# Two transformer blocks on one core: the elementwise work of GpSimd is given to VectorE

## The reference, cut to what matters

```
shift, scale, gate = split(c @ mod_w + mod_b, 3)
h = rms_norm(x, w0) * (1 + scale) + shift
x = x + gate * rms_norm(part(h), w1)          # part: mixer_ab, swiglu, mixer_cd, swiglu
```

## Time and profile before

| | |
|---|---|
| median of three runs | 1168.1 us |
| profiled execution, first to last instruction | 1171.9 us (no other time of it is given) |
| busy: TensorE, VectorE, ScalarE, GpSimd | 1064.7, 807.0, 509.4, 292.7 us |
| low parts on VectorE (line 1003) | 182, 296.7 us in all |
| low parts on GpSimd (line 621) | 91, 242.0 us in all |
| shared jobs on GpSimd (line 654) | 7, 24.0 us in all |
| pair sums on GpSimd (line 471) | 22, 17.8 us in all |

### The profile page before, as it was taken

How to read it: one execution, slowest core, us unless ns; L and a number is a source line. 1 busy time by engine, 2 the same in 40 slices (tenths; PEclk the granted TensorE clock), 3 DMA queues, 4 the chain that set the end, 5 groups by cost and what they waited for, 6 DMA issues and landing times.

```text
span 1171.9 us, 20802 instructions
## 1 busy us (share of the span) xinstructions
PE 1064.7 (91%) x8107; PEld 1010.4 (86%) x8107; DVE 807.0 (69%) x1043; ACT 509.4 (43%) x859; POOL 292.7 (25%) x128
## 2 busy tenths in 40 slices
PE   1788799989999998999979999998989789999996
PEld 1687677979999997988979999997977789999995
DVE  4771657676777756768776777756596687667765
ACT  1421255345444344546344344444641345555454
POOL 2220134122323332220123223331210122232222
PEclk9898799899999999999989999999995899999999
DMA  9889532336677762880527776763753245544540
GB/s 380 284 270 167 187 140 83 92 142 244 254 288 272 266 218 100 294 331 14 178 74 252 270 290 250 265 215 117 253 209 114 95 169 172 184 162 162 180 159 36
DMA packets 58410, 229.44 MB, mean 196 GB/s; under 512 B 6384, under 2 KB 8432, under 8 KB 57840
## 3 DMA queue, kind: packets, MB, share of 16 engines
q1 hardware_dynamic: 58352, 228.64, 56.2%
HBM read 227.04 MB, written 1.57 MB: 195 GB/s over the span
## 4 chain that ended last, share of the span: by engine, by line
PE 58%; DVE 18%; ACT 9%; DMA 7%; issue 6%; SPq 1%; POOL 0%; DVEq 0%; ACTq 0%; POOLq 0%
PE bank L1562 15%; PE bank L1564 14%; PE bank L1563 14%; DMA modbuf<-in_mod_w 5%; DVE wL L1003 4%; DVE acc L485 4%; ACT wH L703 3%; DMA raw<-in_weights 2%; PE bank L1578 2%; PE bank L1648 2%; ACT pr L802 2%; DVE pr L1191 1%; PE bank L1796 1%; PE bank L1678 1%; PE bank L1765 1%
## 5 line engine op out<-in xcount | busy, mean ns | idle before, releaser
L1562 PE MATMUL bank<-hH,wH 128*128 128x256 f32 x1632 | 472.4, 289 | 18.3 <-DVE hL L1051 14.0
L1563 PE MATMUL bank<-hL,wH 128*128 128x256 f32 x1632 | 464.7, 285 | 0.0
L1564 PE MATMUL bank<-hH,wL 128*128 128x256 f32 x1632 | 464.5, 285 | 0.0
L621 POOL TENSOR_TENSOR wL<-raw,wH 128x1024 fp32r<-128x1024 f32 x91 | 242.0, 2659 | 748.4 <-ACT wH L703 748.4
L1003 DVE TENSOR_TENSOR wL<-raw,wH 128x1024 fp32r<-128x1024 f32 x182 | 296.7, 1660 | 90.6 <-ACT wH L703 90.4
L1562 PEld LDWEIGHTS bank<-hH,wH 128*128 128x128 f32 x1632 | 316.1, 194 | 28.0 <-issue 16.5
L1563 PEld LDWEIGHTS bank<-hL,wH 128*128 128x128 f32 x1632 | 316.5, 194 | 0.2
L1564 PEld LDWEIGHTS bank<-hH,wL 128*128 128x128 f32 x1632 | 316.1, 194 | 0.0
L703 ACT ACTIVATE wH<-raw 128x1024 fp32r<-128x1024 f32 x273 | 273.5, 1048 | 79.6 <-PE bank L1564 46.3
L1562 PE MATMUL bank<-aH,wH 128*128 128x256 f32 x528 | 149.5, 283 | 2.1 <-DVE aL L1202 2.1
L1563 PE MATMUL bank<-aL,wH 128*128 128x256 f32 x528 | 149.4, 283 | 0.0
(11 more groups left out here) (237 smaller groups left out, 1186.0 us busy)
## 6 DMA issues: line engine op xcount, KB each, us to landing
raw<-in_weights SPq DMA_DIRECT2D x273, 512.0 KB, 4.6
modbuf<-in_mod_w SPq DMA_DIRECT2D x48, 768.0 KB, 5.1
modbuf<-in_w_ada SPq DMA_DIRECT2D x32, 768.0 KB, 5.3
modbuf<-in_mod_w SPq DMA_DIRECT2D x14, 512.0 KB, 9.6
strips<-in_cmp_w SPq DMA_DIRECT2D x4, 512.0 KB, 10.9
strips<-bias_table SPq DMA_DIRECT2D x8, 256.0 KB, 11.3
otok<-in_mod_w SPq DMA_DIRECT2D x3, 512.0 KB, 15.4
acc<-in_mod_w SPq DMA_DIRECT2D x2, 512.0 KB, 11.2
```

Source lines behind the costliest of these rows:

```text
L621: nc.gpsimd.tensor_tensor(wL[:, slot, :], raw[:, slot, :], wH[:, slot, :].bitcast(F32), ALU.subtract).then_inc(lo_ready[2], 1)
L1562: mm(out, lhs_h, rhs_h, start=start, stop=False, skip_group_check=True)
L1563: mm(out, lhs_h, rhs_l, start=False, stop=False, skip_group_check=True)
L1564: return mm(out, lhs_l, rhs_h, start=False, stop=stop, skip_group_check=True)
```

## The change

GpSimd keeps its clearing and loses the rest. `split_upto` on VectorE makes the low parts of all three classes, and the loop's step makes the third one behind `aL`, ahead of the job. `add_pairs` runs over all four chunks on VectorE; for A0 it stands before the last starting job. The seven shared jobs are ordinary jobs, one in every third step of the attention, behind `take_pt` and `add_o`; ScalarE's `scale_half` goes. GpSimd's `split_low`, `pairs` and its part of the jobs are taken out. No load, no matmul and no buffer is changed.

```diff
         def jobs_done(phase, e):
             if phase == "ab":
-                return JOBS_AT_START + min(KT, e + 1) + min(SHARED_JOBS[0], max(0, e - 9))
+                return JOBS_AT_START + min(KT, e + 1) + min(4, max(0, e - 9))
...
-        def add_pairs(eng, tensor_tensor, norm, chunks=range(4)):
+        def add_pairs(eng, tensor_tensor, norm):
             n = NORMS.index(norm)
-            for b in chunks:
+            for b in range(4):
                 buf = squares_buffer(n, b)
                 eng.wait_ge(sq_ready, 4 * n + b + 1)
-                if b == 3:
-                    eng.wait_ge(pair_ready, 4 * n + 3)
                 tensor_tensor(buf[:, 0:S], buf[:, 0:S], buf[:, S:2 * S], ALU.add).then_inc(pair_ready, 1)
...
         def _(pool):
-            def split_low(b, i=None):
...
-            for n in SHARED_JOBS:
-                q = JOBS_END[0] + n
-                _, _, col, width = JOBS[q]
-                pool.wait_ge(job_scaled, 2 * (n - SHARED_JOBS[0] + 1))
-                pool.wait_ge(mod_used, q)
-                acc = acc0[:, col:col + width]
-                nc.gpsimd.tensor_tensor(acc, acc, modbuf[:, q % 2, :], ALU.add).then_inc(mod_used, 1)
...
             for a in range(2, 24):
                 act.wait_ge(pt_psum, a - 1)
                 exp_rows(a, a % 2)
-                if a % 3 != 1 and halves:
-                    scale_half(*halves.pop(0))
...
             def split_upto(n):
                 while lo.at < min(n, N_UNITS):
-                    if lo.at % 3 != 2:
-                        split_low(lo.at)
+                    split_low(lo.at)
                     lo.at += 1
...
                 if a > 0:
-                    add_pairs(dve, V.tensor_tensor, f"A{a}", (3,))
+                    add_pairs(dve, V.tensor_tensor, f"A{a}")
...
                     V.tensor_tensor(aL[:, t % 2, :], sn[:, t % 2, S:2 * S], aH[:, t % 2, :].bitcast(F32),
                                     ALU.subtract).then_inc(aL_ready, 1)
+                    if split:
+                        split_low(b + 2, i)
                     if jobs:
...
+            jobs_upto(JOBS_AT_START - 1)
+            add_pairs(dve, V.tensor_tensor, "A0")
             jobs_upto(JOBS_AT_START)
...
                 if s >= 10:
                     add_o((s - 10) // 8, (s - 10) % 8)
+                if s % 3 == 2:
+                    jobs_upto(min(lo.job + 1, JOBS_END[1] - 5))
...
-            lo.job = JOBS_END[0] + SHARED_JOBS[-1] + 1
```

More of the change, by code:

```diff
@@ L270, in build_program @@
         mod_used = sem("mod_used")
-        job_scaled = sem("job_scaled")
         acc_zero = sem("acc_zero")
@@ L403, in build_program @@
         assert JOBS_END[-1] == len(JOBS)
-        SHARED_JOBS = range(4, 11)
         def jobs_done(phase, e):
             if phase == "ab":
-                return JOBS_AT_START + min(KT, e + 1) + min(SHARED_JOBS[0], max(0, e - 9))
+                return JOBS_AT_START + min(KT, e + 1) + min(4, max(0, e - 9))
             at = JOBS_END[2 if phase == "cd" else 4]
@@ L615, in _ @@
         def _(pool):
-            def split_low(b, i=None):
[L618 to L622, removed]
             nc.gpsimd.memset(strips[:, :, :], 0.0).then_inc(cw_zero, 1)
             nc.gpsimd.memset(epst[:, :], EPS).then_inc(eps_ready, 1)
[L627 to L635, removed]
             def zero_acc1():
                 nc.gpsimd.memset(acc1, 0.0).then_inc(acc_zero, 1)
[L640 to L646, removed]
-            for n in SHARED_JOBS:
-                q = JOBS_END[0] + n
-                _, _, col, width = JOBS[q]
-                pool.wait_ge(job_scaled, 2 * (n - SHARED_JOBS[0] + 1))
-                pool.wait_ge(mod_used, q)
-                acc = acc0[:, col:col + width]
-                nc.gpsimd.tensor_tensor(acc, acc, modbuf[:, q % 2, :], ALU.add).then_inc(mod_used, 1)
-            plain(6, f0 + 1)
-            pairs("A1")
             wait_y(pool, "ab", 3)
             zero_acc1()
[L660 to L665, removed]
             wait_y(pool, "cd", 3)
             zero_acc1()
[L668 to L677, removed]
         @block.scalar
@@ L856, in _ @@
                                          scale=-1.0).then_inc(gate_exp, 1)
[L857 to L867, removed]
             for a in range(2, 24):
```

## The result

The changed kernel takes 1153.95 us (median of 4 runs, 1149.33 to 1156.70) against 1169.48 us for the kernel before (4 runs): a ratio of 0.985, 95% interval 0.9809 to 0.9891. It is faster, by 15.5 us where 24 were forecast. The two profiled executions span 1171.9 and 1153.9 us, 18.0 us apart. One of the four runs of the low parts alone (1164.38 us) and two of the seventeen of the kernel before measured beside it (1195.23 and 1196.86 us) are slow ones.

A forecast was written before the change was run, and what follows sets the result against it. TensorE was taken to bound the first block's loop, while elsewhere it waits, with GpSimd's time partly paid by VectorE. Terms summed to -23.8 us: 1168.1 becomes 1144.3, said as 1144; own range 1136 to 1150, wider range 1136 to 1162.

The forecast's parts named there:

- the norms over 1.5 us longer: Sign of being wrong: x-to-rstd stretches of the norms over 1.5 us longer.
- VectorE's total hardly moves; the result hangs on the path: VectorE gets about 132 us of work and loses 81 us of standing on low parts, some 50 on others.
- the rival of a full VectorE: VectorE is full, its stretching its own; f2 grows by one low part a turn, 25 us: 1193; chance 0.03.
- the rival of late jobs: In f0 and f1 late job transfers make VectorE's round longer than TensorE's step, 53 us: 1197; chance 0.09.
- f2 -7.4: Last feed-forward loop: 17 turns of 9.09 us fall to TensorE's 8.65, gaining 7.4 us.
- the ring named: In f2 ScalarE and VectorE wait on each other, 9.09 us a turn; the new ring would need 7.9.
- Attention -2.5 and -5.7: First mixer's attention: -2.5 us over twenty steps, and -5.7 from the clock not falling to half behind them.
- the rival that the clock falls all the same: Low clock still comes after the first mixer's attention, the 5.7 us is lost: 1150.0; chance 0.20.
- Start, projections, first and third output stage: Start +1.2 us; projections -2.4 each in first and third mixer, 0 in the middle; output stages -2.5 and -3.0.
- the rival that transfers hide these ends: First and third mixer's projections and three output stages wait for weights arriving no sooner: 1156.9; chance 0.20.
- Second output stage -2.3: Second mixer's output stage: stretched jobs feed transfers that keep their length, so only the first 2.3 us count.
- Norms +3.2: Pair sums now follow the last update of x: +0.5 us each for A1 to A5, +0.7 for A6.

The follow-up runs named there:

- the low parts alone: Kernel before with all low parts made by VectorE, pair sums and shared jobs still as they were: 1150.67 us, ratio 0.9847.
- the scratch subtraction: Changed kernel plus, in f2, a GpSimd subtraction of scratch tiles in each step but the first, read and awaited by nobody: 1182.18 us, ratio 1.0076.
- the part alone: Changed kernel with the third low part of each step back on GpSimd in f2 alone: 1159.53 us, ratio 0.989.
- the run with the jobs alone: Kernel before with only the seven shared jobs of the first attention moved to VectorE: 1166.24 us, ratio 0.9952.
- with the clock held: Changed kernel with TensorE's filler matmuls in norms A1 to A4 raised from 6 to 20: 1148.84 us, ratio 0.9819.
- the run with the memset: Changed kernel plus, in f2, a GpSimd memset of 128x2816 scratch columns behind a one-column subtraction: 1151.89 us, ratio 0.9828.
- that kernel: Changed kernel with VectorE's pair sums of norms A1 to A6 set between its updates of x: 1139.33 us, once more 1140.67 us.

## Why the prediction was right, and what it mis-sized

The time lies in the stated range, but outside the forecast's own, 1136 to 1150. The wider range was there for two rivals that did not come, and what it took in was a miss of another kind: that was luck. Of the signs of being wrong one did show, the norms over 1.5 us longer. The main mechanism, GpSimd's time paid a second time by VectorE, was right.

*VectorE's total hardly moves; the result hangs on the path.* Right: 787.5 us for 807.0, and the scratch subtraction shows that the standing comes from GpSimd's instruction itself. The prediction's subtraction for the low parts gives 77 us and not 81 (81 goes by 182 times their mean of 1660 ns). In all, 132 us of work for 19.5 us less of busy time makes some 150 us of standing, where 131 were put. That excludes the rival of a full VectorE; the rival of late jobs did not come either: f0 and f1 became 0.3 us shorter, and the 50.9 us that VectorE's jobs there waited for transfers are 0.0 now.

*f2 -7.4.* Measured -8.6, by the ring named, as the part alone shows. Most turns are at 8.54 and 8.74 us by turns, 8.64 in the mean, TensorE's (72 matmuls 0.12 us apart: a unit has 24 matmuls, eight groups of three, and not 24 groups). The first three are at 7.66 to 7.99, hence 8.50 in the mean of seventeen. These turns gain 9.9 us, and the last four lose 1.3 of it.

*Attention -2.5 and -5.7.* Measured -3.3 and -4.4. TensorE's fillers at the start of its steps 13, 14, 22 and 23 in the changed kernel, beside the earlier trace rows:

```profile
172.53 0.66 PE L1612 MATMUL bank<-con 128*128 128x128 f32 x4
175.53 0.66 PE L1612 MATMUL bank<-con 128*128 128x128 f32 x4
195.08 0.66 PE L1612 MATMUL bank<-con 128*128 128x128 f32 x4
198.33 0.66 PE L1612 MATMUL bank<-con 128*128 128x128 f32 x4
```

3.00 and 3.25 us for a step of 2.445: waits of 0.56 and 0.81 us, against 0.6 to 0.7 forecast. They come behind the jobs of VectorE's steps 11 and 20, the two named: a job holds up the minimum of the next step, and with it the softmax that TensorE transposes. The second lies behind the twenty steps and so in the other term; the sum, -7.7 for -8.2, is right, and the rival that the clock falls all the same did not come in this place.

*Start, projections, first and third output stage.* Each within 0.9 us of its row (the first output stage's own terms, -2.2, -1.7 and +1.2, add up to -2.7 and not to -2.5); the rival that transfers hide these ends fell. For the start and the first mixer's projections the closeness is partly luck: up to the attention it is 145.67 us in the profile compared, and 141.54 to 145.45 in ten others with the same instructions up to there (147.64 before). Six low parts before the last residual take 6.90 us, the figure forecast:

```profile
930.16 6.90 DVE L933 TENSOR_TENSOR wL<-raw,wH 128x1024 fp32r<-128x1024 f32 x6
```

*Second output stage -2.3.* Measured -6.9. ScalarE's copy of its last unit, before and in the changed kernel:

```profile
584.56 1.06 ACT L703 ACTIVATE wH<-raw 128x1024 fp32r<-128x1024 f32 x1 [3.98 <-DMA raw<-in_weights]
579.26 1.06 ACT L646 ACTIVATE wH<-raw 128x1024 fp32r<-128x1024 f32 x1 [3.73 <-DMA raw<-in_weights]
```

It comes 19.5 us behind the stage's first matmul, 23.6 before (584.56 less 560.93): the transfers, kept at their length as I said, closed up by 4.1 and not by 2.3. The DMA share fits this: it fell to 0.56 (574 to 576 us) and 0.63 (578 to 580 us) before, and is at 0.79 or more from 565 to 577 us now. The rest lies behind the copy, before:

```profile
585.99 3.36 DVE L1003 TENSOR_TENSOR wL<-raw,wH 128x1024 fp32r<-128x1024 f32 x1
589.83 2.04 PE L1578 MATMUL bank<-sq,con 128*128 128x256 f32 x4 [5.64 <-DVE sq L471]
```

The last low part stood behind one of GpSimd that began at 585.69, which makes 1.0 us of the difference. TensorE waited 5.64 us, and the norm's sums behind that ran at the low clock (2.04 us for four matmuls, 1.10 now): 1.8 us. In the run with the jobs alone, whose GpSimd still has its low parts, VectorE's was the first of the two by 0.09 us and took 1.22 us, and the stage took 30.04 us instead of 33.19. From the copy to the rstd it took 7.06 us there, 9.56 before and 6.78 in the changed kernel. So some 2.5 us of the 6.9 hung on which engine began first, as far as one execution can show.

*Norms +3.2: the step that failed.* The +0.5 for each of A1 to A4 became +2.2, +3.4, +2.4 and +1.3; A6 +2.2 for +0.7. The order was seen (pair, sum, square, pair once more), and with the clock held it costs 0.7. What was missed is that the same order makes TensorE stand 3.55 us and that its clock falls behind that, the very mechanism that I had priced in the attention.

*Nothing was forecast for the second attention.* Its +5.6 us are the low clock, which comes and goes there in executions of one kernel. Norms and this make 14.4 us more in the profile than forecast; the larger gains (-6.9, -8.6, -1.3 in the third attention) give 7.1 back. That the medians differ by 15.5 and not 18.0 is of the executions profiled.

## What to carry to other kernels

A short VectorE instruction with two SBUF operands and an odd length, ending together with one of GpSimd, says that GpSimd's time is being paid twice: price the move by what VectorE stops losing, not by what it adds. Then place each moved instruction where its engine was waiting, not behind a block of updates; here the place was worth 11 us (1151.84 against 1140.67) and the engine nothing that the times show. And wherever an order change lets TensorE stand for some us, price what follows at the low clock as well.

## What was not expected of the hardware

The standing goes both ways: in the run with the memset, GpSimd's subtraction of one column took 1.15 us beside a low part of VectorE that had started 0.13 us earlier, and the scratch subtraction 3.36 us, where an f2 low part of the same shape, back on GpSimd, took:

```profile
951.91 2.41 POOL L627 TENSOR_TENSOR wL<-raw,wH 128x1024 fp32r<-128x1024 f32 x1 [375.13 <-ACT wH L663]
```

The granted clock was 1.00 in one execution and 0.50 in another over the same matmuls of the second attention (34.58 and 40.29 us), with the same waits of TensorE ahead (0.32, 0.72 to 0.73 and 0.40 us). Norm A3 of that kernel is another case: behind the same waits of 1.37 and 0.52 us the clock fell in the first profile (10.69 us) and not in the second (9.28). So behind waits of this size it comes and goes, where behind 3.55 us it fell every time. What decides it, no run here shows. The four kernels profiled first among the experiments had 34.6 us in that attention and the four profiled last 37.3 to 40.3, so the hour is not excluded either.
